# A hybrid decoder trunk on one core: in the down projections, most pieces of four weight granules are rounded by one instruction of 2048 elements and subtracted by one instruction of 2048 elements

## The chip, the core and the metric

The kernel runs on one core of a Trainium2 chip. The metric is the device time of one execution in microseconds (us). Engines are named as in the profile: PE is TensorE (PEld its weight loads), ACT is ScalarE, DVE is VectorE, POOL is GpSimd, SP is the queue that issues the DMAs.

## The reference

The program computes two decoder layers for 256 positions of width 2048 in float32. Each layer has a token mixer and a cross-attention over one input projection, an output projection, a layernorm, and a gated feed-forward part, which is the one that matters here:

```python
def _conv_ffn(x, w_up, conv_w, conv_b, w_down):
    h = x @ w_up                                   # 2048 -> 2 * 5632
    hp = jnp.pad(h, ((0, 0), (CONV_WIDTH - 1, 0), (0, 0)))
    hc = conv_b + sum(conv_w[kk] * hp[:, kk:kk + S] for kk in range(CONV_WIDTH))
    gate, up = hc[..., :D_FF], hc[..., D_FF:]
    return (jax.nn.silu(gate) * up) @ w_down       # 5632 -> 2048, the down projection

x = _layernorm(DEEPNORM_ALPHA * x + f, ln2_g[i], ln2_b[i])
```

## The kernel before

**Split weights.** Every large product is made in three matmuls of a rounded 32-bit type: rounded weight times rounded activation, rounded weight times the rest of the activation, and the rest of the weight times rounded activation (`product3`, L1556 to L1560). So each weight that comes from memory as f32 is split on the chip: ACT copies it to the rounded type (`hi_granule`, L531, writes `w_hi`), and DVE subtracts that from the raw weight (`lo_granule`, L939, writes `w_lo`).

**Granules, pieces, chunks.** A granule is 128 rows by 512 columns of a weight. Four granules are a piece, which SP loads with one DMA of 1 MB into one of four slots of `raw`. A down projection is four chunks of 512 output columns, with 11 pieces, 44 granules, each (`s_down0` for layer 0, `s_down1` for layer 1). The split weights have two halves of four granules each; piece k goes into half (half0 + k) mod 2. As 11 is odd, piece 0 of a chunk goes into the half that piece 10 of the chunk before it had, and piece 1 into the other (`split_free`).

**Who waits for whom.** PE waits for one granule at a time (`lo_made`) and counts one granule at a time (`granule_used`); a granule of the down projection is two token tiles by three matmuls of 512 columns. ACT writes granule j of piece k as soon as PE is done with granule j of piece k-2 (of piece 0 and 1 in a chunk: see above). DVE writes the rest of it as soon as ACT has counted it (`hi_made`). SP loads a slot again once DVE has split what was in it (`slot_split`, a wait on `lo_made`).

**Beside the split.** When a chunk of 512 output columns is complete, DVE adds it to the residual and takes statistics (`resid_out`: two instructions at L983, one at L988, two at L990). Its place in the program order of DVE is written out by hand: in chunks 1 and 2, a hardware loop over c with `proj_chunk` as body, it stands between piece 0 and piece 1 of the next chunk; in chunk 3, in `last_proj_chunk`, it stood before the last granule of piece 1. In chunk 0, pieces 0 to 3 share ACT and DVE with the end of the convolution (`taps`, `conv_bank`, `product`, `act_hi_part`, `act_lo_part`). PE's order in the chunks is `tokens_chunk` and, for chunk 3, `last_tokens_chunk`, in which the last three pieces (`HELD`) are gone through twice, and the last piece lies in a place of its own (`is_held`).

```python
def proj_chunk(st, c):
    lo_piece(st, c, 0)
    resid_out(st, c - 1)
    for k in range(1, st.pieces):
        lo_piece(st, c, k)
```

Of the kernel before, what the change touches and what calls it, by code (L numbers as in the profile page):

```python
# [15 lines left out]
F32 = mybir.dt.float32  # L16
F32R = mybir.dt.float32r
I32 = mybir.dt.int32
ALU = mybir.AluOpType
ACT = mybir.ActivationFunctionType  # L20
# [23 lines left out]
PIECE = 4  # L44
SLOTS = 4
# [9 lines left out]
HELD = 3  # L55
# [124 lines left out]
def build(nc, a):  # L180
    ctx = ExitStack()

    def sb(name, shape, dt=F32, stack=ctx):
        return stack.enter_context(nc.sbuf_tensor(name, shape, dt))

    def sem(name):
        return ctx.enter_context(nc.semaphore(name))
# [3 lines left out]
    raw = sb("raw", [P, SLOTS, PIECE * CHUNK])  # L191
    w_hi = sb("w_hi", [P, HALVES * PIECE, CHUNK], F32R)
    w_lo = sb("w_lo", [P, HALVES * PIECE, CHUNK], F32R)
# [5 lines left out]
    def region(name, parts):  # L199

        stack = ExitStack()
        made = [sb(f"{name}_{n}", shape, dt, stack) for n, shape, dt in parts]
        stack.close()
        return made
# [4 lines left out]
    xT, _, act = region("ffn", [split_x, margin, ("act", [P, FF_T, 2, S], F32R)])  # L209
    _, x_rows = region("tokens", [margin, split_x])  # L210
    _, _, kvbuf, qmT0, _, memT, _, x_raw = region("memory", [
        split_x, margin, ("kv", [P, 8, 512], F32), ("qmT", [P, MEM_HEADS, S], F32), ("moving_margin", [P, MOVING_MARGIN], F32), ("memT", [P, KT, 2, S], F32R),
        ("between", [P, KT, S], F32), ("x", [P, KT, S], F32)])
    first, = region("head", [("first", [P, KT, CHUNK + S], F32)])

    _, _, _, _, _, dT, pool_h, pool_a, pool_b, probs0, _, pool_hi2, pool_lo2 = region("pool", [
        split_x, margin, ("kv", [P, 8, 512], F32), ("qmT", [P, MEM_HEADS, S], F32), ("moving_margin", [P, MOVING_MARGIN], F32), ("dT", [P, MIX_T, 2, S], F32R),
        ("h", [P, 4, PAD + S], F32), ("a", [P, 4, PAD + S], F32), ("b", [P, 4, PAD + S], F32),
        ("probs", [P, 2, TT, S], F32), ("apart", [P, POOL_APART], F32)] + [(f"w_{x}", [P, 2, CHUNK], F32R) for x in ("hi", "lo")])
    _, _, h_tok, qkT, qmT1, kv1, probs1, scores, square, rot = region("diff", [  # L220
        split_x, margin, ("h_tok", [P, TT, DIFF_W], F32), ("qkT", [P, HEADS, 2 * S], F32), ("qmT", [P, MEM_HEADS, S], F32),
        ("kv", [P, 4, 512], F32), ("probs", [P, 2, TT, S], F32),
        ("scores", [P, TT, 2, S], F32), ("square", [P, 2 * TT, P], F32), ("rot", [P, 4, 128], F32)])
# [3 lines left out]
    _, _, _, _, up_hi2, up_lo2 = region("up_pair", [split_x, margin, ("act", [P, FF_T - 2 * PIECE - 5, 2, S], F32R), apart] + pair_split)  # L227
    _, _, _, _, _, _, _, kv_hi2, kv_lo2 = region("kv_head", [
        split_x, margin, ("kv", [P, 8, 512], F32), ("qmT", [P, MEM_HEADS, S], F32), ("moving_margin", [P, MOVING_MARGIN], F32),
        ("memT", [P, KT, 2, S], F32R), ("apart", [P, POOL_APART], F32)] + pair_split)  # L230
    head_split = [(f"w_{x}", [P, HEAD, CHUNK], F32R) for x in ("hi", "lo")]
    _, _, next_hi, next_lo, held_hi, held_lo, turned, rows = region("next", [split_x, margin] + head_split + [
        ("held_" + n, shape, dt) for n, shape, dt in held_split] + [("tokens", [P, TT, CHUNK], F32), ("rows", [P, 2, ROWS], F32)])
    _, _, _, next_raw = region("next_from", [split_x, margin, head_split[0], ("raw", [P, HEAD, CHUNK], F32)])
    out_gb, _, last_hi, last_lo = region("last", [("gb", [P, 2, D], F32), margin] + held_split)
# [54 lines left out]
    def raw_place(st, c, k, j):  # L290

        if from_first(st, c):
            return first[:, PIECE * k + j, 0:CHUNK]
        if is_head(st, c, k):
            return next_raw[:, PIECE * k + j, :]
        return raw[:, k % SLOTS, j * CHUNK:j * CHUNK + st.width]

    def split_place(st, c, k, j):

        if is_head(st, c, k):  # L300
            return next_hi[:, PIECE * k + j, :], next_lo[:, PIECE * k + j, :]
        if is_held(st, c, k):
            hi, lo = (last_hi, last_lo) if st is s_down1 else (held_hi, held_lo)
            return hi[:, j, :], lo[:, j, :]
        if apart_at(st, c, k, j):
            hi, lo = split_apart[st][0:2]
            return hi[:, j % 2, :], lo[:, j % 2, :]
        at = st.split_at(k, j)
        return w_hi[:, at, 0:st.width], w_lo[:, at, 0:st.width]

    def bank(b, lo, hi):
        if isinstance(b, int):
            return acc[:, b, lo:hi]
        return acc[:, bass.ds(b, 1), lo:hi].rearrange("p a n -> p (a n)")
# [20 lines left out]
    s_out, s_up, s_down = (s_out0, s_out1), (s_up0, s_up1), (s_down0, s_down1)  # L335
    normed_streams = (s_up0, s_diff, s_up1)

    piece_loaded = [sem(f"piece_loaded{s}") for s in range(SLOTS)]
    hi_made = sem("hi_made")
    lo_made = sem("lo_made")  # L340
    granule_used = sem("granule_used")
# [173 lines left out]
    def _(act_e):  # L515
        def hi_granule(st, c, k, j):
            if j == 0 and is_head(st, c, k):
                act_e.wait_ge(head_loaded[k], 16 * (normed_streams.index(st) + 1))
            elif j == 0 and not from_first(st, c):
                act_e.wait_ge(piece_loaded[k % SLOTS], st.loaded(c, k))  # L520
            hi, _ = split_place(st, c, k, j)
            free = st.split_free(c, k, j)
            if st in normed_streams and isinstance(c, int) and c == 0:
                free = head_free(st) if is_head(st, c, k) else st.granule(0, 0, 0)
            if st in s_up and apart_at(st, c, k, j):
                free = s_out[s_up.index(st)].used(0)
            if is_held(st, c, k):
                free = st.used(0) if st in s_out else s_down0.granule(3, 6, 0) if st is s_down0 else s_up1.used(2 * FF_CHUNKS - 1)
            if not (isinstance(free, int) and free <= 0):
                act_e.wait_ge(granule_used, free)  # L530
            nc.scalar.activation(hi, raw_place(st, c, k, j), ACT.Copy).then_inc(hi_made, 1)  # L531

        def hi_piece(st, c, k):
            for j in range(PIECE):
                hi_granule(st, c, k, j)

# [19 lines left out]
        def first_chunk(st, l, n):  # L556
# [22 lines left out]
            if (l, n) == (0, 0):  # L579
                act_e.wait_ge(kv1_stored, 16)  # L580
            hi_piece(st, 0, 0)
            hi_piece(st, 0, 1)

            root_table()
# [97 lines left out]
        for n in range(16):  # L682
            c, k = n // 4, n % 4
            for j in range(PIECE):
                i = PIECE * n + j
                if i == 0:
                    hi, raw_w = split_place(s_kv, 0, 0, 0)[0], raw_place(s_kv, 0, 0, 0)
# [35 lines left out]
        for n in range(16):  # L723
            c, k = n // 4, n % 4
# [28 lines left out]
        for l in range(DEPTH):  # L753
# [97 lines left out]
            with nc.scalar.Fori(1, 3) as c:  # L851
                for k in range(4):
                    hi_piece(s_out[l], c, k)
# [71 lines left out]
    def _(dve):  # L925
# [10 lines left out]
        def lo_granule(st, c, k, j):  # L936
            dve.wait_ge(hi_made, st.granule(c, k, j) + 1)
            hi, lo = split_place(st, c, k, j)
            nc.vector.tensor_tensor(lo, raw_place(st, c, k, j), hi.bitcast(F32), ALU.subtract).then_inc(lo_made, 1)  # L939

        def lo_piece(st, c, k):
            for j in range(PIECE):
                lo_granule(st, c, k, j)

# [33 lines left out]
        def resid_out(st, c):  # L978

            dve.wait_ge(granule_used, st.used(c))  # L980
            for t in range(TT):
                cols = x_tok[:, t, bass.ds(c * CHUNK, CHUNK)]
                order.then(nc.vector.scalar_tensor_tensor(cols, cols, ALPHA, bank(2 * c + t, 0, CHUNK), ALU.mult, ALU.add))  # L983
            order.wait()
            def row(t, at):
                return stats[:, t, bass.ds(at, 1), :].rearrange("p a n -> p (a n)")

            order.then(nc.vector.bn_stats(row(0, c), x_tok[:, 0, bass.ds(c * CHUNK, CHUNK)]))  # L988
            for half in range(2):
                order.then(nc.vector.bn_stats(row(1, c * 2 + half), x_tok[:, 1, bass.ds(c * CHUNK + half * HALF, HALF)]))  # L990
# [7 lines left out]
        def last_proj_chunk(st):  # L998

            lo_piece(st, 3, 0)  # L1000
            for j in range(PIECE - 1):
                lo_granule(st, 3, 1, j)
            resid_out(st, 2)
            lo_granule(st, 3, 1, PIECE - 1)
            for k in range(2, st.pieces):
                lo_piece(st, 3, k)

# [230 lines left out]
        for n in range(16):  # L1238
            c, k = n // 4, n % 4
# [88 lines left out]
        for n in range(16):  # L1328
            c, k = n // 4, n % 4
# [670 lines left out]
```

## Time and profile before

| | |
|---|---|
| time, median of 3 runs | 2101.45 us (2100.76 to 2101.49) |
| span of the profiled execution | 2098.4 us (its own time is not listed apart; the median is 3.05 us above the span) |
| PE busy | 2092.7 us, 100% |
| DVE busy | 1385.1 us, 66% |
| ACT busy | 1167.7 us, 56% |
| DMA, share of 16 engines | 55.9%, 195 GB/s |
| down projection of layer 0 | about 773 to 1013 us of the span |
| down projection of layer 1 | about 1848 to 2088 us of the span |

Busy time counts an engine's running instructions; idle time is put down to the event that ended it. A matmul's row shows its whole pass through the array (0.39 us for 512 columns), while the next one starts 0.23 us after it: the distance of the starts is the pace. Idle time of an engine that nobody waits for costs nothing.

### The profile page before, as it was taken

Reading aid. Unit: us, or ns where it says so; the run is one execution under the profiler, and the core shown is the slowest. Engines: PE = TensorE matmul, PEld = TensorE weight load, DVE = VectorE, ACT = ScalarE, POOL = GpSimd, SP = SyncE. Lnnn points to the kernel's source line nnn. Section 1 sums busy time; section 2 is a strip of 40 time slices with the busy share of each in tenths; the row PEclk is TensorE's granted clock in tenths of the full one; section 3 lists DMA queues with packets and bytes.
Section 4 is the critical chain, followed back from the end, with each engine's and each line's share of the span. In section 5 each row is a group of like instructions: output and inputs, shape, how many; then the busy total and the mean of one; then the engine's idle time right before and its main releaser. Section 6 shows DMA issues by size and latency. Waiting matters only on the chain.

```text
span 2098.4 us, 38433 instructions
## 1 busy us (share of the span) xinstructions
PE 2092.7 (100%) x14108; PEld 1910.5 (91%) x14108; DVE 1385.1 (66%) x2477; ACT 1167.7 (56%) x2129; POOL 2.7 (0%) x12
## 2 busy tenths in 40 slices
PE   9999999999999999999999999999999999999999
PEld 9999889999999998888888888899999999988887
DVE  5767677767676675455756558667776676755555
ACT  5655556555565554444656666565565555644443
POOL 0000000000000000000000000000000000000000
PEclk9999999999999999999999999999999999999999
DMA  9654666555555555556544445645555555466552
GB/s 349 238 168 165 220 211 211 201 185 186 205 183 200 194 181 185 200 180 221 195 168 163 169 169 178 243 153 195 205 189 200 188 186 205 161 240 215 186 199 101
DMA packets 201616, 408.76 MB, mean 195 GB/s; under 512 B 7616, under 2 KB 9152, under 8 KB 200768
## 3 DMA queue, kind: packets, MB, share of 16 engines
q1 hardware_dynamic: 201392, 407.45, 55.9%
q8 instruction: 48, 0.79, 0.2%
q14 instruction: 32, 0.26, 0.0%
q10 hardware_dynamic: 144, 0.26, 0.0%
HBM read 404.53 MB, written 3.15 MB: 194 GB/s over the span
## 4 chain that ended last, share of the span: by engine, by line
PE 99%; DVE 1%; ACT 0%; issue 0%
PE acc L1558 32%; PE acc L1560 32%; PE acc L1559 32%; PE acc L1855 0%; PE acc L1732 0%; PE acc L1829 0%; PE acc L1646 0%; PE acc L1698 0%; PE acc L1713 0%; PE acc L1879 0%; PE acc L1639 0%; PE acc L1887 0%; DVE x_tok L1529 0%; PE acc L1758 0%; PE acc L1725 0%; DVE x_tok L1534 0%
## 5 line engine op out<-in xcount | busy, mean ns | idle before, releaser
L939 DVE TENSOR_TENSOR w_lo<-raw,w_hi 128x512 fp32r<-128x512 f32 (+1 forms) x1422 | 941.8, 687 | 582.3 <-ACT w_hi L531 580.9
L531 ACT ACTIVATE w_hi<-raw 128x512 fp32r<-128x512 f32 (+1 forms) x1422 | 865.9, 629 | 687.7 <-PE acc L1560 679.2
L1558 PE MATMUL acc<-ffn_xT,w_hi 128*128 128x256 f32 x2920 | 806.9, 276 | 0.0
L1559 PE MATMUL acc<-ffn_xT,w_hi 128*128 128x256 f32 x2920 | 806.0, 276 | 0.0
L1560 PE MATMUL acc<-ffn_xT,w_lo 128*128 128x256 f32 x2920 | 806.0, 276 | 0.0
L1559 PEld LDWEIGHTS acc<-ffn_xT,w_hi 128*128 128x128 f32 x2920 | 548.2, 188 | 0.2
L1558 PEld LDWEIGHTS acc<-ffn_xT,w_hi 128*128 128x128 f32 x2920 | 548.2, 188 | 0.2
L1560 PEld LDWEIGHTS acc<-ffn_xT,w_lo 128*128 128x128 f32 x2920 | 548.1, 188 | 0.0
L1559 PE MATMUL acc<-w_lo,ffn_act 128*128 128x512 f32 x688 | 267.6, 389 | 0.0
L1560 PE MATMUL acc<-w_hi,ffn_act 128*128 128x512 f32 x688 | 267.6, 389 | 0.0
L1558 PE MATMUL acc<-w_hi,ffn_act 128*128 128x512 f32 x688 | 267.6, 389 | 0.0
L1558 PE MATMUL acc<-w_hi,tokens_xT 128*128 128x512 f32 x544 | 216.2, 397 | 0.0
L1560 PE MATMUL acc<-w_hi,tokens_xT 128*128 128x512 f32 x544 | 212.2, 390 | 0.0
L1559 PE MATMUL acc<-w_lo,tokens_xT 128*128 128x512 f32 x544 | 211.9, 389 | 0.0
L1154 DVE SCALAR_TENSOR_TENSOR conv<-acc,table,conv 128x255 f32<-128x255 f32 (+1 forms) x352 | 153.2, 477 | 37.5 <-ACT conv L653 25.6
L1558 PEld LDWEIGHTS acc<-w_hi,ffn_act 128*128 128x128 f32 x688 | 129.1, 188 | 26.9
L1560 PEld LDWEIGHTS acc<-w_hi,ffn_act 128*128 128x128 f32 x688 | 129.1, 188 | 26.8
L1559 PEld LDWEIGHTS acc<-w_lo,ffn_act 128*128 128x128 f32 x688 | 129.1, 188 | 26.6
L1560 PEld LDWEIGHTS acc<-w_hi,tokens_xT 128*128 128x128 f32 x544 | 102.1, 188 | 21.7
L1559 PEld LDWEIGHTS acc<-w_lo,tokens_xT 128*128 128x128 f32 x544 | 102.3, 188 | 20.2
L1558 PEld LDWEIGHTS acc<-w_hi,tokens_xT 128*128 128x128 f32 x544 | 102.2, 188 | 20.2
L653 ACT ACTIVATE conv<-acc,table 128x256 f32<-128x256 f32 x176 | 84.4, 559 | 10.7 <-PE acc L1560 9.6
(276 smaller groups left out, 1333.3 us busy)
## 6 DMA issues: line engine op xcount, KB each, us to landing
raw<-in_ffn_w_up SPq DMA_DIRECT2D x172, 1024.0 KB, 4.9
raw<-in_ffn_w_down SPq DMA_DIRECT2D x88, 1024.0 KB, 5.1
raw<-in_diff_w_in SPq DMA_DIRECT2D x38, 1024.0 KB, 5.1
raw<-in_w_out SPq DMA_DIRECT2D x32, 1024.0 KB, 5.1
raw<-in_pool_w_in SPq DMA_DIRECT2D x16, 1024.0 KB, 5.2
raw<-in_mem_w_kv SPq DMA_DIRECT2D x12, 1024.0 KB, 12.7
next_from_raw<-in_ffn_w_up SPq DMA_DIRECT2D x4, 1024.0 KB, 10.6
head_first<-in_first SPq DMA_DIRECT2D x5, 768.0 KB, 10.8
```

Of the source, the lines that this page charges most:

```text
L531: nc.scalar.activation(hi, raw_place(st, c, k, j), ACT.Copy).then_inc(hi_made, 1)
L653: ins = nc.scalar.activation(conv[:, s, b, f * S:(f + 1) * S], acc[:, 2 * s + b, f * S:(f + 1) * S], ACT.Identity, bias=table[:, l, bass.d ...
L939: nc.vector.tensor_tensor(lo, raw_place(st, c, k, j), hi.bitcast(F32), ALU.subtract).then_inc(lo_made, 1)
L1154: ins = nc.vector.scalar_tensor_tensor(to, acc[:, 2 * s + b, f * S:(f + 1) * S - lag], table[:, l, bass.ds(col, 1)], to, ALU.mult, ALU.add)
L1558: pe.matmul(out, w[0], x[0], start=start, stop=False, skip_group_check=True)
L1559: pe.matmul(out, w[0], x[1], start=False, stop=False, skip_group_check=True)
L1560: return pe.matmul(out, w[1], x[0], start=False, stop=stop, skip_group_check=True)
```

## The change

In the down projections (`is_wide`) one ACT instruction rounds the four granules of a piece, 2048 elements per partition, and one DVE instruction subtracts them. It is so for pieces 4 to 10 of chunk 0, 1 to 10 of chunks 1 and 2, and 1 to 7 of chunk 3, 34 pieces per layer, 68 in all. The wide ACT instruction waits until the half it writes is free as a whole (`PIECE - 1`), and counts four on `hi_made` at its end; the wide DVE instruction waits for that, and counts four on `lo_made` at its end. PE's program is as before: it still waits granule by granule. In `last_proj_chunk` the residual of chunk 2 now stands behind the whole of piece 1. The other projections are as before.

```diff
+    def is_wide(st, c, k):
+
+        return st in s_down and k > 0 and (k >= SLOTS or not (isinstance(c, int) and c == 0)) and (k < st.pieces - HELD or not (isinstance(c, int) and c == 3))
+
+    def wide_split(st, k):
+
+        at = st.split_at(k, 0)
+        return (x[:, at:at + PIECE, :].rearrange("p j n -> p (j n)") for x in (w_hi, w_lo))
...
         def hi_piece(st, c, k):
+            if is_wide(st, c, k):
+                act_e.wait_ge(piece_loaded[k % SLOTS], st.loaded(c, k))
+                act_e.wait_ge(granule_used, st.split_free(c, k, PIECE - 1))
+                hi, _ = wide_split(st, k)
+                nc.scalar.activation(hi, raw[:, k % SLOTS, :], ACT.Copy).then_inc(hi_made, PIECE)
+                return
...
         def lo_piece(st, c, k):
+            if is_wide(st, c, k):
+                dve.wait_ge(hi_made, st.granule(c, k, PIECE - 1) + 1)
+                hi, lo = wide_split(st, k)
+                nc.vector.tensor_tensor(lo, raw[:, k % SLOTS, :], hi.bitcast(F32), ALU.subtract).then_inc(lo_made, PIECE)
+                return
...
             lo_piece(st, 3, 0)
-            for j in range(PIECE - 1):
-                lo_granule(st, 3, 1, j)
-            resid_out(st, 2)
-            lo_granule(st, 3, 1, PIECE - 1)
+            if is_wide(st, 3, 1):
+                lo_piece(st, 3, 1)
+                resid_out(st, 2)
+            else:
+                for j in range(PIECE - 1):
+                    lo_granule(st, 3, 1, j)
+                resid_out(st, 2)
+                lo_granule(st, 3, 1, PIECE - 1)
```

The order of DVE's instructions at two places. The first is the loop over chunks 1 and 2 of the down projection of layer 0, from the end of `resid_out` (`stats`, `x_tok`) to the first split of piece 1. Before:

```order
L988 ISA
L988 BN_STATS stats<-x_tok 128x6
L990 ISA
L990 BN_STATS stats<-x_tok 128x6
L990 ISA
L990 REGISTER_ALU
L990 BN_STATS stats<-x_tok 128x6
L937 REGISTER_ALU
L939 TENSOR_TENSOR w_lo<-raw,w_hi 128x512
```

And in the changed kernel (its lines are numbered anew):

```order
L1008 ISA
L1008 BN_STATS stats<-x_tok 128x6
L1010 ISA
L1010 BN_STATS stats<-x_tok 128x6
L1010 ISA
L1010 REGISTER_ALU
L1010 BN_STATS stats<-x_tok 128x6
L958 REGISTER_ALU
L960 TENSOR_TENSOR w_lo<-raw,w_hi 128x2048
```

The residual has kept its place; what stands behind it is four granules in one instruction instead of the first of four. The second place is chunk 3 of the same layer (straight code), before:

```order
L939 TENSOR_TENSOR w_lo<-raw,w_hi 128x512 x7
L983 SCALAR_TENSOR_TENSOR x_tok<-x_tok,acc 128x512 x2
L988 BN_STATS stats<-x_tok 128x6
L990 BN_STATS stats<-x_tok 128x6 x2
L939 TENSOR_TENSOR w_lo<-raw,w_hi 128x512 x33
L939 TENSOR_TENSOR next_held_w_lo<-raw,next_held_w_hi 128x512 x4
```

And in the changed kernel:

```order
L954 TENSOR_TENSOR w_lo<-raw,w_hi 128x512 x4
L960 TENSOR_TENSOR w_lo<-raw,w_hi 128x2048
L1003 SCALAR_TENSOR_TENSOR x_tok<-x_tok,acc 128x512 x2
L1008 BN_STATS stats<-x_tok 128x6
L1010 BN_STATS stats<-x_tok 128x6 x2
L960 TENSOR_TENSOR w_lo<-raw,w_hi 128x2048 x6
L954 TENSOR_TENSOR w_lo<-raw,w_hi 128x512 x8
```

Here the residual has moved from behind the third granule of piece 1 to behind its fourth.

## Rows read from the trace of the kernel before

**Rows 1.** The page: busy time of PE, and the chain that ended last.

```profile
PE 2092.7 (100%) x14108; PEld 1910.5 (91%) x14108; DVE 1385.1 (66%) x2477; ACT 1167.7 (56%) x2129; POOL 2.7 (0%) x12
...
PE 99%; DVE 1%; ACT 0%; issue 0%
```

**Rows 2.** Timeline in the middle of chunk 1: start, duration, engine, instruction, [idle before].

```profile
843.78 0.63 ACT L531 ACTIVATE w_hi<-raw 128x512 fp32r<-128x512 f32 x1 [0.73 <-PE acc L1560]
...
844.45 0.69 DVE L939 TENSOR_TENSOR w_lo<-raw,w_hi 128x512 fp32r<-128x512 f32 x1 [0.67 <-ACT w_hi L531]
```

**Rows 3.** Groups by form, 512 and 1024 elements: count, busy us, mean ns, idle before.

```profile
L531 ACT ACTIVATE w_hi<-raw 128x512 fp32r<-128x512 f32 x1410 | 860.4, 630 | 685.3 <-PE acc L1560 676.8 <-DMA raw<-in_mem_w_kv 7.5 <-DMA raw<-in_w_out 0.9
...
L720 ACT ACTIVATE pool_dT<-pool_h 128x1024 fp32r<-128x1024 f32 x3 | 3.2, 1063 | 7.1 <-DVE pool_h L1285 7.1
...
L939 DVE TENSOR_TENSOR w_lo<-raw,w_hi 128x512 fp32r<-128x512 f32 x1410 | 935.6, 688 | 581.4 <-ACT w_hi L531 580.1
...
L1313 DVE TENSOR_TENSOR pool_dT<-pool_h,pool_dT 128x1024 fp32r<-128x1024 f32 x3 | 3.7, 1221 | 0.2 <-issue 0.2
```

**Rows 4.** Timeline of ACT and of DVE where chunk 1 follows on chunk 0.

```profile
832.90 3.76 ACT L531 ACTIVATE w_hi<-raw 128x512 fp32r<-128x512 f32 x7 [0.73 <-PE acc L1560]
...
833.57 0.69 DVE L939 TENSOR_TENSOR w_lo<-raw,w_hi 128x512 fp32r<-128x512 f32 x1 [0.67 <-ACT w_hi L531]
834.17 1.28 DVE L983 SCALAR_TENSOR_TENSOR x_tok<-x_tok,acc  x2
...
836.87 3.08 DVE L939 TENSOR_TENSOR w_lo<-raw,w_hi 128x512 fp32r<-128x512 f32 x5
```

**Rows 5.** Timeline of PE and PEld: first matmul of pieces 0 and 1 of chunk 1.

```profile
832.70 0.39 PE L1558 MATMUL acc<-w_hi,ffn_act 128*128 128x512 f32 x1
...
837.92 0.19 PEld L1558 LDWEIGHTS acc<-w_hi,ffn_act 128*128 128x128 f32 x1
...
838.14 0.39 PE L1558 MATMUL acc<-w_hi,ffn_act 128*128 128x512 f32 x1
```

**Rows 6.** Timeline where PE waits for DVE, near the end of the program.

```profile
2091.04 0.75 DVE L1529 SCALAR_TENSOR_TENSOR x_tok<-x_tok,mean_var,last_gb 128x512 f32<-128x512 f32 x1
...
2091.91 0.30 PEld L1960 LDWEIGHTS acc<-x_tok,conv 128*128 128x128 f32 x2 [1.21 <-ACT conv L905]
2091.94 1.10 PE L1960 MATMUL acc<-x_tok,conv 128*128 128x512 f32 x2 [0.41 <-DVE x_tok L1529]
```

**Rows 7.** Timeline where chunk 3 follows on chunk 2: ACT, PEld of piece 1.

```profile
952.58 3.76 ACT L531 ACTIVATE w_hi<-raw 128x512 fp32r<-128x512 f32 x7 [0.73 <-PE acc L1560]
...
957.60 0.19 PEld L1558 LDWEIGHTS acc<-w_hi,ffn_act 128*128 128x128 f32 x1
```

**Rows 8.** Timeline of SP and ACT; tile `next_from_raw`: its loads' landing (all six).

```profile
981.89 0.93 SPq L406 DMA_DIRECT2D next_from_raw<-in_diff_w_in  x2
...
998.72 4.27 ACT L531 ACTIVATE next_w_hi<-next_from_raw 128x512 fp32r<-128x512 f32 x8
...
DMA to landing us min/median/max: 7.1/10.5/12.3
```

**Rows 9.** Windows: PE, PEld, DVE, ACT, POOL busy (x), granted clock, DMA share, GB/s.

```profile
823.00:828.00 5.00, 5.00 (x24) 4.14 (x23) 0.38 (x1) 0.00 (x0) 0.00 (x0) 1.00 0.62 208
843.00:848.00 5.00, 5.00 (x24) 4.14 (x23) 2.77 (x4) 2.09 (x5) 0.00 (x0) 1.00 0.99 348
...
2091.00:2092.00 1.00, 0.59 (x3) 0.09 (x1) 0.96 (x3) 0.40 (x1) 0.00 (x0) 1.00 0.68 256
2093.00:2098.00 5.00, 1.13 (x3) 0.30 (x2) 1.53 (x3) 1.20 (x2) 0.00 (x0) 0.81 0.58 210
```

**Rows 10.** Timeline of PE at the program's start.

```profile
1.06 3.78 PE L1758 MATMUL acc<-conv 128*128 128x128 f32 x16 [1.06 <-DVE conv L1174]
4.53 2.05 PE L1732 MATMUL acc<-memory_memT,kv_head_w_hi 128*128 128x256 f32 x8
...
7.20 1.10 PE L1732 MATMUL acc<-memory_memT,kv_head_w_hi 128*128 128x256 f32 x8
```

## The prediction

> **What bounds the kernel now.** I read the page first. PE is busy for the whole span, and the chain that ended last is PE for 99% of it [rows 1]. So whatever is taken from ACT, DVE or SP gives nothing unless PE's pace changes with it, and whatever makes PE wait is added in full, since no later slack exists in which PE could catch up. The question is only: does PE find its split weights in time?
>
> Next the timeline inside a down projection. PE takes a piece, four granules, in 838.14 - 832.70 = 5.44 us [rows 5]. In the middle of a chunk ACT and DVE each sleep before every granule, ACT 0.73 us until PE frees a place, DVE 0.67 us until ACT is through; DVE starts 0.04 us after ACT's end (844.45 against 843.78 + 0.63) [rows 2]. The splitting runs well ahead of PE.
>
> Then the one tight place, where one chunk follows on another. Call T the start of PE's first matmul of piece 0 of the new chunk, 832.70 [rows 5]. ACT can round the last granule of that piece at 832.90, T + 0.20, and goes on with piece 1 at once, one granule each (3.76 - 0.63) / 6 = 0.52 us. DVE splits the last granule of piece 0 at 833.57, then does the residual of the chunk before, from 834.17 to 836.87, 2.70 us, and only then begins on piece 1 [rows 4]. PEld loads the first weights of piece 1 at 837.92 [rows 5]. DVE's first granule is ready at 836.87 + 0.69 = 837.56, 0.36 us before that, and the three behind it follow faster than PE's 1.36 us each. The old order fits, barely, because the first granule is all that PE needs there.
>
> **The wide instructions by themselves.** No row shows 2048 elements. ACT takes 630 ns for 512 and 1063 for 1024, DVE 688 and 1221 [rows 3]. Carried on by the same slope, 0.846 ns per element on ACT gives 1063 + 1024 x 0.846 = 1.93 us, and 1.041 on DVE gives 1221 + 1024 x 1.041 = 2.29 us. The far bound is four times the narrow one, 2.52 and 2.75 us. I take the slope, since rows of 512 and 1024 lie on it, and keep the other end for a rival.
>
> Per wide piece, ACT is busy less than four times 630 ns and DVE less than four times 688 ns. I count that at nothing: both slept anyway [rows 2]. The Trainium skill, "VectorE: DVE Perf Modes", section on the TRN2 errata, says that memory latency is exposed between instructions, so one large tile pays it once and many small ones each time. By that rule the merge is a gain; by the rows the gain falls into idle time.
>
> **Wide pieces in the middle of a chunk.** ACT now waits until the half is free as a whole, T + 0.20 for the piece two further on. From there 1.93 + 0.04 + 2.29 us, and then PE must see it. The nearest row for PE waiting on DVE: DVE ends at 2091.04 + 0.75 = 2091.79, PEld starts at 2091.91, 0.12 us later [rows 6]. Ready at T + 4.58; PEld wants it at 837.92 - 832.70 = T + 5.22 [rows 5]. **Slack 0.64 us, cost 0**; the cover is PE's one piece in between, and what is lost if it goes stands under the rivals. In chunk 0 DVE has the end of the convolution beside pieces 0 to 3, which stay narrow; its first wide piece, 4, starts from the same wait.
>
> **Chunks 1 and 2, after the residual.** The residual keeps its place. ACT's wide instruction begins at the pace of its queue, 832.90 + 0.52 = 833.42, and ends at 835.35, before DVE asks. DVE starts at 836.87 as before, but now delivers all four granules at once: 836.87 + 2.29 = 839.16. With 0.12 us the load is at 839.28 instead of 837.92, 1.36 us late. Some of that may come back: a matmul normally starts 838.14 - 837.92 = 0.22 us after its load, and after a wait 0.03 us (2091.91 to 2091.94) [rows 5, 6], so by its starts PE is late by 839.31 - 838.14 = 1.17 us. Bounds: 839.16 - 838.14 = 1.02 us if the signal costs nothing, 1.36 if nothing comes back. I take 1.25, between the last two, as the matmul after a wait has to sit behind its load. This happens at the start of chunks 1 and 2 in two layers: **4 x 1.25 = +5.0 us** (4.1 to 5.4). Behind it nothing more is late: piece 2 is ready by T + 5.64 + 1.93 + 0.04 + 2.29 + 0.12 = T + 10.0, and PE wants it at T + 5.22 + 1.25 + 5.44 = T + 11.9.
>
> **Chunk 3.** Here the residual now stands behind piece 1. ACT begins its wide instruction at 952.58 + 0.52 = 953.10; + 1.93 + 0.04 + 2.29 + 0.12 = 957.48, and PEld wants it at 957.60 [rows 7]. **Cost 0, but with 0.12 us to spare**; the pessimistic end is a few tenths, twice. Then the residual, from 957.36 for 2.70 us [rows 4], and the wide piece 2 after it, ready at 960.06 + 2.29 + 0.12 = 962.47; PEld wants it at 957.60 + 5.44 = 963.04. Nobody else waits for the residual early. So this chunk holds the same work as the other two in the other order, and should not stall.
>
> **Loads.** A slot of `raw` is free when DVE has split the whole piece. That was 0.20 + 0.63 + 0.04 + 0.69 = 1.56 us after the start of the piece before, and is now 4.46: 2.9 us later. It hits SP's queue, in which the loads for the next projection stand behind those of chunk 3. They were issued at 981.89; 2.9 us later and with the longest landing of 12.3 us they are there at 997.1, and ACT first reads them at 998.72 [rows 8]. Within the chunks a load has some three pieces of time. Cost 0.
>
> **Sum.** Span 2098.4 + 5.0 = 2103.4 us. The median of the runs lies 3.05 us above the span, so 2101.45 + 5.0 = **2106.5 us**, 0.24% slower. Changes within 0.2%, 4.2 us, are about what a measurement of this kernel cannot tell from none; my sum stands just outside.
>
> **Rivals.**
>
> *PE's pace rises (the other side).* If ACT's and DVE's accesses slow PE's reading, fewer instructions could let it go faster. The wide pieces are 68 x 5.44 = 370 us of PE, so from 1.4% on, 3 ns per matmul, the stalls are paid back; at 3% the kernel is at 2101.45 + 5.0 - 11.1 = 2095.4. Against it: with ACT asleep and DVE nearly so, PE did 24 matmuls in 5 us, and 24 with both at work [rows 9]; what moves is also the same number of bytes. It is also where the quoted errata rule would have to lead if it were to help. Chance 4%; a smaller gain that just makes it "no change" is in there.
>
> *The stall is shorter than I think.* At 1.02 us each the sum is 4.1 us, 2105.5, inside 0.2%. It needs no mistake in the mechanism, only in the 0.12 us and in what comes back. Chance 18%, and 5% more that it is smaller still, because DVE reaches its wide instruction sooner.
>
> *The wide instructions cost four narrow ones.* Then a piece is ready at T + 0.20 + 2.52 + 0.04 + 2.75 + 0.12 = T + 5.63, 0.41 us late. Some 62 pieces inside chunks give 25 us, the four boundaries 4 x 1.7 = 7 us, chunk 3 about 2 x 0.9 = 2 us: 2135. It decides from 0.64 us more for both together. Against it: the slope [rows 3]. Chance 4%.
>
> *The clock falls after a stall.* At the program's start 8 matmuls of 256 columns took 2.05 us, from 7.20 on 1.10 us: half pace, for up to 7.20 - 1.06 = 6.1 us [rows 10]. If every stall were followed by such a stretch, each would lose another 3 us: 2106.5 + 12 = 2118.5. Against it: PE's idle 0.41 us [rows 6] left the granted clock at 1.00, and it fell, to a mean of 0.81, only in the last 5 us, with PE busy for 1.13 of them [rows 9]; a stall of 1.25 us stands between 10 us stretches of full work. The Trainium skill, "TensorE: Matmul & The Clock Gate", Part 1, has idleness as what takes the clock to half; no row here shows it for a gap this short. Chance 4%.
>
> *Chunk 3 stalls too,* or piece 1 is later by a few tenths: 2107 to 2108.5. Chance 12%.
>
> **How the numbers follow.** The forecast as it stands, 2105.7 to 2107, has 53%. With its two neighbours, the shorter stall and chunk 3, the cases from 2105 to 2108.5 hold 83%. For 8 in 10 with the errors of these terms I give 2104.0 to 2109.0; outside are the pace, the wide cost, the clock, and part of the smaller stalls. Slower by over 0.2% (above 2105.65): 53 + 12 + 4 + 4 = 73%. Within 0.2%: 18 + 5 and half of the pace rival, 25%. Faster: 2%.
>
> **What would show it.** In the trace of the changed kernel: wide ACT near 1.93 us and wide DVE near 2.29 us, 68 each; PE idle four times, once per loop pass of each layer, in front of the first matmul of piece 1 and released by DVE; no PE idle time at the start of chunk 3, and none inside chunks; granted clock 1.00 throughout; PE's pace still 5.44 us a piece. I am wrong if PE shows many short waits spread over the chunks, if it shows none and the time is the old one, or if a wait's cost isn't near 1.2 us.

## The result and the profile after

| | before | changed |
|---|---|---|
| median of 10 runs each | 2100.71 us (2099.93 to 2101.49) | 2105.81 us (2105.24 to 2106.41) |
| ratio | | 1.0023, 95% interval 1.0015 to 1.0031 |
| span of the profiled execution | 2098.4 us | 2104.3 us |

The changed kernel is 5.1 us slower, 0.23% by the ratio of the runs. That is just outside the 0.2% that I had taken as the bound of what can be told from no change; the interval excludes 1, but its lower end lies inside the 0.2%. The profiled execution itself took 2106.08 us, 1.8 us more than its span.

The page of the changed kernel comes first, with its busy times:

```profile
PE 2094.6 (100%) x14108; PEld 1910.3 (91%) x14108; DVE 1356.9 (64%) x2273; ACT 1128.9 (54%) x1925; POOL 2.7 (0%) x12
```

DVE is busy 28.2 us less than in [rows 1], ACT 38.8 us less, each with 204 instructions fewer (68 wide ones in place of 272). None of it shows in the time. The next fence has the groups by form of the changed kernel, with the two new forms (count, busy us, mean ns, idle before); they stand against the rows of 512 and 1024 elements in [rows 3].

```profile
L960 DVE TENSOR_TENSOR w_lo<-raw,w_hi 128x2048 fp32r<-128x2048 f32 x68 | 155.8, 2291 | 190.9 <-ACT w_hi L547 190.6
L547 ACT ACTIVATE w_hi<-raw 128x2048 fp32r<-128x2048 f32 x68 | 130.2, 1915 | 221.6 <-PE acc L1584 221.6
```

The wide subtraction takes 2.29 us, as extrapolated; the wide copy 1.92 us instead of 1.93. Then the waits: who waited for whom, us in total, times, longest. The kernel before has these of PE:

```profile
PE acc L1758 <- DVE conv L1174: 1.1, 1, 1.1
PE acc L1960 <- DVE x_tok L1529: 0.6, 2, 0.4
```

And the changed kernel has these, first PE's, then the largest of PEld's:

```profile
PE acc L1582 <- DVE w_lo L960: 3.6, 4, 0.9
PE acc L1782 <- DVE conv L1198: 1.1, 1, 1.1
PE acc L1984 <- DVE x_tok L1553: 0.6, 2, 0.4
PE acc L1582 <- DVE w_lo L954: 0.4, 1, 0.4
...
PEld acc L1582 <- DVE w_lo L960: 5.3, 4, 1.3
```

The waits for `conv` and for `x_tok` are the old ones. Four are new and are for a wide subtraction (L960). The one of 0.4 us for L954 is at 14.2 us, in the program's first loads, far ahead of the change. This is one of the four, where chunk 1 follows on chunk 0, in the timeline; it answers to [rows 4, 5].

```profile
834.62 1.91 ACT L547 ACTIVATE w_hi<-raw 128x2048 fp32r<-128x2048 f32 x1
...
835.36 1.28 DVE L1003 SCALAR_TENSOR_TENSOR x_tok<-x_tok,acc  x2
...
838.04 2.27 DVE L960 TENSOR_TENSOR w_lo<-raw,w_hi 128x2048 fp32r<-128x2048 f32 x1
...
839.09 0.39 PE L1584 MATMUL acc<-w_hi,ffn_act 128*128 128x512 f32 x1
...
840.37 0.19 PEld L1582 LDWEIGHTS acc<-w_hi,ffn_act 128*128 128x128 f32 x1 [1.31 <-DVE w_lo L960]
840.37 0.50 PE L1582 MATMUL acc<-w_hi,ffn_act 128*128 128x512 f32 x1 [0.89 <-DVE w_lo L960]
840.71 0.40 PE L1583 MATMUL acc<-w_lo,ffn_act 128*128 128x512 f32 x1
...
845.97 0.39 PE L1582 MATMUL acc<-w_hi,ffn_act 128*128 128x512 f32 x1
```

ACT's wide instruction ends at 836.53 and waits for nobody; DVE is in the residual until 838.04, then takes 2.27 us over all four granules, and the weight load starts 0.06 us after DVE's end. PE's first matmul of piece 1 starts 1.05 us late (840.37 against 839.09 + 0.23), and the piece then takes 845.97 - 840.37 = 5.60 us instead of 5.44, because the second matmul starts 0.34 us after the first instead of 0.23 and the next few are slightly slow too. What the whole wait costs is read from the distance of chunks: ACT rounds the last granule of piece 0 at 834.08 here, at 895.13 in chunk 2 and at 956.15 in chunk 3.

```profile
834.08 0.63 ACT L540 ACTIVATE w_hi<-raw 128x512 fp32r<-128x512 f32 x1 [0.73 <-PE acc L1584]
...
895.13 0.63 ACT L540 ACTIVATE w_hi<-raw 128x512 fp32r<-128x512 f32 x1 [0.73 <-PE acc L1584]
...
956.15 0.63 ACT L540 ACTIVATE w_hi<-raw 128x512 fp32r<-128x512 f32 x1 [0.73 <-PE acc L1584]
```

So chunk 1 takes 61.05 us and chunk 2 61.02. The kernel before needed 11 x 5.44 = 59.84 us for each: (952.58 - 832.90) / 2 = 59.84 [rows 4, 7]. **Each wait costs 1.2 us, four of them 4.8 us.** The two parts above, 1.05 and 0.16, add up to the same.

The stretch from the first matmul of layer 0's down projection to the last of layer 1's says it once more (count, shortest/median/longest in ns, first and last start). Before:

```profile
L1558 PE MATMUL acc<-w_hi,ffn_act x688: 389/389/392, 772.8 to 2084.4; 128*128 128x512 f32 x172
...
L1560 PE MATMUL acc<-last_w_hi,ffn_act x11: 282/283/389, 2077.4 to 2087.8; 128*128 128x256 f32 x6, 128*128 128x512 f32 x5
```

And in the changed kernel:

```profile
L1582 PE MATMUL acc<-w_hi,ffn_act x688: 389/389/499, 774.0 to 2090.3; 128*128 128x512 f32 x172
...
L1584 PE MATMUL acc<-last_w_hi,ffn_act x11: 283/283/389, 2083.3 to 2093.7; 128*128 128x256 f32 x6, 128*128 128x512 f32 x5
```

That is 2087.8 - 772.8 = 1315.0 us before and 2093.7 - 774.0 = 1319.7 us now, 4.7 us more. The rest of the difference of the spans, 5.9 - 4.7 = 1.2 us, is there before the change begins: the first of these matmuls already starts at 774.0 instead of 772.8. It builds up in the first 50 us: ACT's first copy starts at 4.27 us instead of 3.97, and its copies to `memory_kv` start 0.77 and then 1.2 us late. The edit touches nothing there, and in the runs below the same matmul starts between 773.0 and 776.0. Why this part differs from one trace to the next stays open; it is not a cost of the wide instructions. The stretch leaves it out, so it tells small differences better than the medians do.

### The profile page after: what moved, and what is told of

It reads as the page before. It is cut to its first block, busy times and chain, and to the rows that moved or that the text cites. A ratio compares the mean times of both kernels' runs of the same rounds, so it can differ in the third digit from the quotient of the medians.

```text
span 2104.3 us, 37893 instructions
## 1 busy us (share of the span) xinstructions
PE 2094.6 (100%) x14108; PEld 1910.3 (91%) x14108; DVE 1356.9 (64%) x2273; ACT 1128.9 (54%) x1925; POOL 2.7 (0%) x12
## 4 chain that ended last, share of the span: by engine, by line
PE 97%; DVE 1%; DMA 0%; issue 0%; ACT 0%; SPq 0%; DVEq 0%
PE acc L1582 32%; PE acc L1584 31%; PE acc L1583 31%; PE acc L1879 0%; DVE w_lo L960 0%; DMA head_first<-in_first 0%; PE acc L1853 0%; PE acc L1670 0%; PE acc L1722 0%; PE acc L1737 0%; PE acc L1903 0%; PE acc L1663 0%; PE acc L1911 0%; DVE x_tok L1553 0%; DVE x_tok L1003 0%
## 5 line engine op out<-in xcount | busy, mean ns | idle before, releaser
L954 DVE TENSOR_TENSOR w_lo<-raw,w_hi 128x512 fp32r<-128x512 f32 x1150 | 757.8, 686 | 425.2 <-ACT w_hi L540 424.5
L540 ACT ACTIVATE w_hi<-raw 128x512 fp32r<-128x512 f32 x1150 | 698.0, 629 | 508.5 <-PE acc L1584 502.8
L960 DVE TENSOR_TENSOR w_lo<-raw,w_hi 128x2048 fp32r<-128x2048 f32 x68 | 155.8, 2291 | 190.9 <-ACT w_hi L547 190.6
L547 ACT ACTIVATE w_hi<-raw 128x2048 fp32r<-128x2048 f32 x68 | 130.2, 1915 | 221.6 <-PE acc L1584 221.6
L1584 PEld LDWEIGHTS acc<-w_hi,tokens_xT 128*128 128x128 f32 x544 | 102.1, 188 | 21.7
```

The lines of the kernel that those rows point to most:

```text
L547: nc.scalar.activation(hi, raw[:, k % SLOTS, :], ACT.Copy).then_inc(hi_made, PIECE)
L960: nc.vector.tensor_tensor(lo, raw[:, k % SLOTS, :], hi.bitcast(F32), ALU.subtract).then_inc(lo_made, PIECE)
L1584: return pe.matmul(out, w[1], x[0], start=False, stop=stop, skip_group_check=True)
```

## The experiments

All of them start from the changed kernel. T is again the start of PE's first matmul of a chunk. The medians and ratios, each against the kernel before on the same chip in the same session, and from each trace the stretch between the first and the last matmul of the two down projections (1315.0 us in the kernel before):

| run | median us | ratio to before | 95% interval | stretch us | PE waits for a wide split |
|---|---|---|---|---|---|
| changed kernel | 2105.81 | 1.0023 | 1.0015 to 1.0031 | 1319.7 | 4 |
| 1. residual behind piece 1 | 2100.30 | 0.9996 | 0.9987 to 1.0005 | 1315.0 | 0 |
| 2. piece 1 narrow | 2100.51 | 1.0000 | 0.9991 to 1.0009 | 1314.9 | 0 |
| 3. only piece 1 wide | 2106.33 | 1.0024 | 1.0015 to 1.0033 | 1319.7 | 4 |
| 4. only DVE wide | 2105.46 | 1.0021 | 1.0012 to 1.0030 | 1319.9 | 4 |
| 5. only ACT wide | 2101.28 | 1.0002 | 0.9993 to 1.0011 | 1315.0 | 0 |
| 6. residual ahead of piece 1 in chunk 3 too | 2108.54 | 1.0036 | 1.0022 to 1.0050 | 1321.8 | 6 |
| 7. 512 elements more per piece | 2107.17 | 1.0030 | 1.0018 to 1.0041 | 1321.8 | 4, and PEld alone in nearly every wide piece |
| 8. 1024 elements more per piece | 2123.19 | 1.0106 | 1.0090 to 1.0121 | 1337.9 | 34 |

**1. The residual behind piece 1.** The theory puts the whole loss on an order: the wide instruction stands behind the residual. Its rival is a small cost in every wide piece.

```diff
         def proj_chunk(st, c):
             lo_piece(st, c, 0)
+            before_resid = 2 if st in s_down else 1
+            for k in range(1, before_resid):
+                lo_piece(st, c, k)
             resid_out(st, c - 1)
-            for k in range(1, st.pieces):
+            for k in range(before_resid, st.pieces):
                 lo_piece(st, c, k)
```

> All wide pieces stay; in chunks 1 and 2 the residual moves behind piece 1, as in chunk 3. Theory (the cost is DVE's wide instruction standing behind the 2.70 us residual, once per loop pass of each layer, four waits of 1.2 us): piece 1 is ready at T + 0.20 + 0.54 + 1.92 + 0.04 + 2.29 + 0.06 = T + 5.05 against T + 5.22 wanted, so no wait is left, and the time is that of the kernel before, 2100.7 us (2100.0 to 2101.7). Rival (the wide instructions cost a little in every one of the 68 pieces): still about 2105.8. A partial rival: the margin of 0.17 us fails and a few tenths per boundary stay, 2101.5 to 2103.

Measured: 2100.30 us, ratio 0.9996, no wait. DVE's timeline at the same boundary, in this kernel:

```profile
834.75 0.69 DVE L954 TENSOR_TENSOR w_lo<-raw,w_hi 128x512 fp32r<-128x512 f32 x1 [0.67 <-ACT w_hi L540]
836.62 2.29 DVE L960 TENSOR_TENSOR w_lo<-raw,w_hi 128x2048 fp32r<-128x2048 f32 x1 [1.18 <-ACT w_hi L547]
838.83 1.27 DVE L1003 SCALAR_TENSOR_TENSOR x_tok<-x_tok,acc  x2
...
839.10 0.19 PEld L1585 LDWEIGHTS acc<-w_hi,ffn_act 128*128 128x128 f32 x1
```

The wide piece 1 is done at 838.91, and PEld loads on time at 839.10: a margin of 0.19 us. DVE slept 1.18 us ahead of it, too short for the 2.70 us of the residual as a whole. All 68 wide pieces are kept and the loss is gone, in the stretch to 0.1 us, so the rival falls. This version is as fast as the kernel before and not faster.

**2. Piece 1 of chunks 1 and 2 narrow again**, the other 64 wide pieces kept.

```diff
         return st in s_down and k > 0 and (...)
+            and (k != 1 or isinstance(c, int))
```

> As the changed kernel, but piece 1 of chunks 1 and 2 is split granule by granule again (64 wide pieces are left). Theory: DVE's first granule behind the residual is ready 0.36 us before it is wanted, no wait, 2100.7 us. Rival (a cost in every wide piece): 64/68 of the loss stays, about 2105.5.

Measured: 2100.51 us, ratio 1.0000, no wait for a split in the down projections. As expected.

**3. Only piece 1 of chunks 1 and 2 wide**, four pieces in the whole program.

```diff
-        return st in s_down and k > 0 and (...)
+        return st in s_down and k == 1 and not isinstance(c, int)
```

> The reverse: only piece 1 of chunks 1 and 2 is wide, 4 pieces in all; everything else is as before the change. Theory: the whole loss comes back, four waits of 1.2 us, 2105.5 us (2105.0 to 2106.2). Rival (a cost in every wide piece): 4/68 of the loss, 2101.0.

Measured: 2106.33 us, ratio 1.0024, with the same line of waits as the changed kernel:

```profile
PE acc L1582 <- DVE w_lo L960: 3.6, 4, 0.9
```

Four instructions out of 68 carry all of the loss. The medians alone, with intervals of 0.09% to each side, would leave room for up to about 2 us from the other 64; the stretches of runs 1, 2 and 3 (1315.0, 1314.9, 1319.7) leave about 0.1 us.

**4. Only DVE wide.** ACT goes back to granules.

```diff
         def hi_piece(st, c, k):
-            if is_wide(st, c, k):
+            if False:
```

> ACT rounds granule by granule as before the change, DVE still subtracts whole pieces. Theory: what is late at piece 1 of chunks 1 and 2 is DVE alone, which starts when the residual is done, by which time four narrow ACT instructions from T + 0.72 to T + 2.9 are long through; so the four waits of 1.2 us stay, 2105.6 us (2105.0 to 2106.3). In the middle of a chunk ACT keeps pace with PE's granules and DVE's start is T + 0.20 + 0.63 + 0.04, 1.3 us earlier than with a wide ACT, no wait. Rival (ACT's long wait for the whole half costs): the loss goes, 2100.7.

Measured: 2105.46 us, ratio 1.0021, four waits of PE. As expected. PEld waits six times, 5.6 us in all; the two more are short and PE doesn't see them. They are where chunk 3 begins, at 960.32 and 2038.40 us. There four ACT instructions at 0.52 us each end later than one wide one, and the thin margin of chunk 3 is used up; the stretch is 0.2 us longer.

**5. Only ACT wide.** DVE goes back to granules.

```diff
         def lo_piece(st, c, k):
-            if is_wide(st, c, k):
+            if False:
```

> ACT rounds whole pieces, DVE subtracts granule by granule. Theory: at piece 1 of chunks 1 and 2 the wide ACT instruction ends at T + 0.74 + 1.91 = T + 2.65, before DVE has ended the residual at T + 4.17; DVE's first granule is ready at T + 4.9, wanted at T + 5.22: no wait, 2100.7 us (2100.0 to 2101.7). In the middle of a chunk the first granule is ready at T + 0.20 + 1.92 + 0.04 + 0.69, far ahead. Rival (ACT's wait for the whole half costs): about 2105.8.

Measured: 2101.28 us, ratio 1.0002 with an interval on both sides of 1, no wait. The median lies inside what was expected, and the stretch is the old one. So it is the wide instruction of DVE, not ACT's wait for a whole half, that costs.

**6. The residual ahead of piece 1 in chunk 3 too.**

```diff
             if is_wide(st, 3, 1):
-                lo_piece(st, 3, 1)
                 resid_out(st, 2)
+                lo_piece(st, 3, 1)
```

> As the changed kernel, but in chunk 3 too the residual stands between piece 0 and the wide piece 1. Theory: two more waits of 1.2 us, so 2105.8 + 2.4 = 2108.2 us (2107.6 to 2108.8), and PE waits six times instead of four. Rival (the order in chunk 3 is of no matter, since the loop around chunks 1 and 2 is what costs): 2105.8.

Measured: 2108.54 us, ratio 1.0036; the interval is wide, 5 runs. PE waits six times:

```profile
PE acc L1582 <- DVE w_lo L960: 5.1, 6, 0.9
```

The median is 2.7 us above the changed kernel's; the stretch, which is the better measure here, is 2.1 us longer, for two waits. They are a little shorter than the other four, 0.77 to 0.78 us of idle PE instead of 0.89. The place of the residual is what decides, also where there is no loop.

**7 and 8. Taking the cover away in the middle of a chunk.** Before each wide subtraction, except those of pieces 1, DVE makes a first part of it once more; the added work changes no value.

```diff
                 hi, lo = wide_split(st, k)
+                if k > 1:
+                    order.done(nc.vector.tensor_tensor(lo[:, 0:n * CHUNK], raw[:, k % SLOTS, 0:n * CHUNK],
+                                                       hi[:, 0:n * CHUNK].bitcast(F32), ALU.subtract))
```

With n = 1, and then with n = 2; the loop's count of `order` steps is raised by the nine added per pass.

> As the changed kernel, but before each wide subtraction, except those of pieces 1, DVE does the first 512 elements of it once more and waits for itself: 0.73 us more on DVE in 62 pieces. This measures how much cover the wide pieces have in the middle of a chunk. In the changed kernel's trace a wide piece is ready about 0.54 us before PEld wants it. Theory: each piece in the middle is now 0.73 - 0.54 = 0.19 us late, and PE can't catch up, so about 58 x 0.19 = 11 us more, 2117 us (2110 to 2124), with PE waiting for DVE at nearly every wide piece. Rival (the cover is larger, or DVE's added work still falls into its idle 3.15 us): no change, 2105.8.

> As the last one, but with 1024 elements more, 1.27 us on DVE. Theory: 1.27 - 0.54 = 0.73 us per piece, 58 x 0.73 = 42 us more than the changed kernel, 2148 us (2140 to 2156); the difference to the run with 512 more is 58 x 0.54 = 31 us, whatever the exact cover. Rival: DVE's added 1.27 us falls into its idle 3.15 us per piece, 2105.8.

Measured: 2107.17 us and 2123.19 us, that is 1.4 us and 17.4 us above the changed kernel, and by the stretch 2.1 us and 18.2 us, where I expected 11 and 42. Two steps of my expectation were wrong. The timeline of the second of these kernels, with 1024 elements more, shows the first:

```profile
848.73 1.92 ACT L547 ACTIVATE w_hi<-raw 128x2048 fp32r<-128x2048 f32 x1 [4.71 <-PE acc L1586]
854.17 1.91 ACT L547 ACTIVATE w_hi<-raw 128x2048 fp32r<-128x2048 f32 x1 [3.52 <-PE acc L1586]
...
850.68 1.23 DVE L961 TENSOR_TENSOR w_lo<-raw,w_hi 128x1024 fp32r<-128x1024 f32 x1 [3.01 <-ACT w_hi L547]
852.01 2.29 DVE L962 TENSOR_TENSOR w_lo<-raw,w_hi 128x2048 fp32r<-128x2048 f32 x1
...
853.46 0.19 PEld L1586 LDWEIGHTS acc<-w_hi,ffn_act 128*128 128x128 f32 x1
854.36 0.19 PEld L1584 LDWEIGHTS acc<-w_hi,ffn_act 128*128 128x128 f32 x1 [0.70 <-DVE w_lo L962]
...
853.68 0.39 PE L1586 MATMUL acc<-w_hi,ffn_act 128*128 128x512 f32 x1
854.36 0.50 PE L1584 MATMUL acc<-w_hi,ffn_act 128*128 128x512 f32 x1 [0.28 <-DVE w_lo L962]
...
865.85 0.50 PE L1584 MATMUL acc<-w_hi,ffn_act 128*128 128x512 f32 x1 [0.28 <-DVE w_lo L962]
```

First, only every second piece makes PE wait: PE stands at 854.36 and next at 865.85, which is 2 x 5.44 + 0.61 us later. ACT starts on the next piece but one, at 854.17, when PE ends the piece before the wait, and so before the wait ends; that piece gets the wait's length as cover, and is on time. The waits of this kernel say the same, 34 of PE, four of them at piece 1, so 30 in the middle of chunks, not 58:

```profile
PE acc L1584 <- DVE w_lo L962: 12.1, 34, 0.9
```

30 x 0.61 = 18 us, which is the 18.2 of the stretch. The cover up to the weight load, 0.54 us in my expectation, was nearly right. In the changed kernel a wide subtraction starts 0.10 us after ACT's end, so here it would have started at 848.73 + 1.92 + 0.10 = 850.75; it starts at 852.01, 1.26 us later. The load comes at 854.36 instead of 853.46 + 0.23, 0.67 us late. So 1.26 - 0.67 = 0.59 us was covered.

The second wrong step is in the kernel with 512 more: I had let PE pay for the whole lateness of a load. Its waits, and its timeline at the load of one piece and of the next:

```profile
PE acc L1584 <- DVE w_lo L962: 3.6, 4, 0.9
...
PEld acc L1584 <- DVE w_lo L962: 10.5, 35, 1.3
```

```profile
853.23 0.19 PEld L1586 LDWEIGHTS acc<-w_hi,ffn_act 128*128 128x128 f32 x1
853.59 0.19 PEld L1584 LDWEIGHTS acc<-w_hi,ffn_act 128*128 128x128 f32 x1 [0.17 <-DVE w_lo L962]
...
858.70 0.19 PEld L1586 LDWEIGHTS acc<-w_hi,ffn_act 128*128 128x128 f32 x1
859.03 0.19 PEld L1584 LDWEIGHTS acc<-w_hi,ffn_act 128*128 128x128 f32 x1
...
853.45 0.39 PE L1586 MATMUL acc<-w_hi,ffn_act 128*128 128x512 f32 x1
853.68 0.41 PE L1584 MATMUL acc<-w_hi,ffn_act 128*128 128x512 f32 x1
```

The load at 853.59 is 0.13 us late, yet its matmul starts on time at 853.68, as loads normally run 0.23 us ahead. What is lost is a few hundredths in the matmuls behind it. As PE hardly moves, the next piece gets no cover either, and its load at 859.03 is late too (0.33 us after the load before it instead of 0.23). The views name no idle time below 0.15 us, so the 35 waits, 31 of them in the middle of chunks, are only the longer ones: by the starts of the loads in the trace, 58 in the middle of chunks have 0.10 to 0.20 us of idle time ahead of them instead of 0.04. Together they cost the 2.1 us, about 0.04 us each.

So the two runs behave differently. In run 7 the loads are late by less than the 0.23 us of their lead: that costs PE little, but happens at every piece. In run 8 they are late by more: that costs PE nearly all of the lateness (0.61 of 0.67 us), but only at every second piece. What lies between the two was not tried.

## Why the prediction was right

**What bounds.** Confirmed: 38.8 us less of ACT and 28.2 us less of DVE gave nothing in any run, since runs 1 and 2, with 68 and 64 wide instructions on both engines, end where the kernel before does. The gain that one would read out of the errata section of "VectorE: DVE Perf Modes" in the Trainium skill is in the trace (DVE is busy 2.29 us for a piece in place of 4 x 0.69) and falls into idle time.

**Wide instructions.** 2.29 and 1.93 us by the slope of 512 and 1024 elements; 2.29 and 1.92 measured.

**The two handovers.** Each was off by 0.06 us, in opposite directions. I had DVE start 0.04 us after ACT's end, as it does with 512 elements; the wide one starts 0.10 us after it. I had the weight load 0.12 us behind DVE's end; it comes 0.06 us behind. Where both stand in one chain, in the middle of a chunk and in chunk 3, the errors cancel, and that was luck. Where the residual holds DVE up, only the second counts.

**Chunks 1 and 2.** The term that makes the forecast, 4 x 1.25 = 5.0 us. There were four waits, at the place named and released by DVE, with 1.2 us each by the length of the chunks, 4.8 in all (4.7 by the stretch). The load was 1.27 us late (840.37 against 839.10), not 1.36, because of the shorter handover. My reason for taking 1.25 instead of the 1.17 by starts was wrong: the matmul after the wait did not sit behind its load but started with it, so by starts only 1.05 us were lost. What brought it back to 1.2 is something that I had not counted, the 0.16 us by which the piece behind the wait ran slower. The mechanism was right; that the size came out within 0.05 us is partly luck. Run 3 makes the term alone.

**Chunk 3.** No wait, as forecast. In the changed kernel's trace DVE ends piece 1 at 958.69 + 2.29 = 960.98 and the load comes at 961.17, on time. After the 0.06 us of the handover, 0.13 us are to spare, where I had 0.12.

```profile
958.69 2.29 DVE L960 TENSOR_TENSOR w_lo<-raw,w_hi 128x2048 fp32r<-128x2048 f32 x1 [1.18 <-ACT w_hi L547]
...
961.17 0.19 PEld L1582 LDWEIGHTS acc<-w_hi,ffn_act 128*128 128x128 f32 x1
```

The margin held in both layers, and in the loop in run 1. It is thin indeed: in run 4 four narrow ACT instructions used it up. Run 6 shows that the order was the reason.

**Middle of a chunk.** Cost 0, as forecast. The margin was 0.64 us in the prediction. In the changed kernel it is 851.18 - (848.25 + 2.29) - 0.06 = 0.58 us, and run 8 has 0.59:

```profile
846.23 1.92 ACT L547 ACTIVATE w_hi<-raw 128x2048 fp32r<-128x2048 f32 x1 [4.74 <-PE acc L1584]
...
848.25 2.29 DVE L960 TENSOR_TENSOR w_lo<-raw,w_hi 128x2048 fp32r<-128x2048 f32 x1 [4.36 <-ACT w_hi L547]
...
851.18 0.19 PEld L1582 LDWEIGHTS acc<-w_hi,ffn_act 128*128 128x128 f32 x1
```

The difference is ACT's start, 0.26 us after the piece's first matmul (846.23 against 845.97) and not 0.20.

**Loads.** The loads for the next projection were to be issued 2.9 us later. They are issued at 988.50 instead of 981.89; 1.2 us of that was there before, 2.4 us are the two waits of this layer, and the 3.0 us that are left fit the slot's late release. ACT reads them at 1002.30 and waits for nothing:

```profile
988.50 0.93 SPq L415 DMA_DIRECT2D next_from_raw<-in_diff_w_in  x2
...
1002.30 4.26 ACT L540 ACTIVATE next_w_hi<-next_from_raw 128x512 fp32r<-128x512 f32 x8
```

**The sum and the rivals.** 2106.5 us was forecast, 2105.81 measured. The 0.7 us between them are the base: the median of the kernel before was 2101.45 in three runs and 2100.71 in ten. The added time, 5.0 against 5.1, agrees. The 3.05 us that the sum sets between span and median are not what an execution takes beyond its span: in all nine later profiled executions that is 1.8 to 2.2 us, so the traced execution of the kernel before was, by my estimate, about 1 us faster than its median. As the term only led back to that median, it did no harm. PE's pace didn't rise: in the middle of chunk 1 ACT's wide instructions, each released by PE, start at 846.23 and 851.67, 5.44 us apart as before, and run 1, with all 68 wide pieces and no wait, has the stretch of the kernel before. Had the wide instructions cost four narrow ones, the rival's 25 us inside the chunks would have been too much: by what run 8 shows, that only every second piece makes PE wait, I estimate about half. Nor did the clock fall: the granted clock reads 1.00 in both chunks with waits, in windows over the changed kernel (PE, PEld, DVE, ACT, POOL busy, clock, DMA share, GB/s):

```profile
830.00:890.00 60.00, 59.11 (x261) 48.59 (x260) 28.13 (x19) 21.58 (x14) 0.00 (x0) 1.00 0.56 190
890.00:950.00 60.00, 59.11 (x261) 48.64 (x260) 28.14 (x19) 21.58 (x14) 0.00 (x0) 1.00 0.56 192
```

The granted clock stayed at the upper of its two levels, 2.4 GHz, and from the second one after the wait on the matmuls are 0.23 to 0.24 us apart. So an idle PE of 0.9 us left the clock alone here. "TensorE: Matmul & The Clock Gate" in the Trainium skill, Part 1, has idleness as what lowers it; the last row of [rows 9] agrees, a mean of 0.81 with PE busy for 1.13 of 5 us. The half pace at the program's start, on which the rival was built, is not in the record of the granted clock, which reads 1.00 there; so these rows don't show that the clock was its cause. Before the change:

```profile
0.00:5.00 5.00, 3.94 (x18) 3.94 (x19) 1.17 (x5) 2.11 (x4) 2.54 (x11) 1.00 0.61 207
```

## What to carry to other kernels

When several small instructions are merged into one, its consumer gets the first result when the last is done. Look for the places where the producer starts late because of other work, here once per chunk: there the merge costs what the consumer has too little of lead, and order can give it back (put the other work behind the merged instruction instead of ahead of it). And merging on an engine that sleeps while another one bounds the kernel buys nothing, however much busy time it takes away.

In a double buffer a delay of the producer need not cost its full length each time: a wait of the consumer gives cover to the piece behind it, so that only every second piece makes it wait. An estimate of "delay minus slack, times pieces" is then twice too high, as in run 8. Where the consumer absorbs most of the lateness, as in run 7, there is no such cover and every piece is late, at little cost.

When two kernels differ by a few microseconds in two milliseconds, compare a stretch between the same two instructions in their traces. Here the part ahead of the change differed by up to 3 us from trace to trace, and the stretch behind it told runs apart to 0.1 us.

## What the runs showed of the hardware

ACT's copy took 630, 1063 and 1915 ns for 512, 1024 and 2048 f32 elements per partition, DVE's subtraction 688, 1221 and 2291 ns, so both go on nearly in a straight line, at 0.83 and 1.04 ns per element from 1024 to 2048. DVE started 0.10 us after the ACT instruction that it waited for when its own instruction had 2048 elements, and 0.03 to 0.04 us after it with 512 or 1024; why is open. A weight load after a wait for DVE started 0.06 us after DVE's end, the matmul started with it, and the next matmul came 0.1 us later than usual. What I had not expected is that loads may be up to about 0.15 us late in nearly every piece, as in run 7, at a cost to PE of about 0.04 us each, because they run 0.23 us ahead of their matmuls.
